# FFN in-projection by Strassen's seven block products from the third body on, out-projection in two halves

## The reference

```
gate, up = split(rms_norm(h, g) @ w_in, 2)      # w_in: 1024 x 5632, gate and up 2816 wide each
h = h + 0.5 * (silu(gate) * up) @ w_out         # w_out: 2816 x 1024
```

## Time and profile before

| | |
|---|---|
| runs of the kernel before (median) | 1895.05 us |
| the profiled execution, own time | 1895.18 us |
| its span, first to last instruction | 1893.4 us |
| TensorE busy | 1866.8 us, 99% |
| weight loads busy (beside TensorE) | 1536.2 us, 81% |
| VectorE busy | 927.1 us, 49% |
| ScalarE busy | 718.8 us, 38% |
| GpSimd busy | 24.5 us, 1% |
| granted TensorE clock, mean | 0.994 |
| DMA | 174.36 MB, 92 GB/s |

### The profile page before, as it was taken

How to read it: one execution, slowest core, us unless ns; L and a number is a source line. 1 busy time by engine, 2 the same in 40 slices (tenths; PEclk the granted TensorE clock), 3 DMA queues, 4 the chain that set the end, 5 groups by cost and what they waited for, 6 DMA issues and landing times.

```text
span 1893.4 us, 24130 instructions
## 1 busy us (share of the span) xinstructions
PE 1866.8 (99%) x8779; PEld 1536.2 (81%) x8779; DVE 927.1 (49%) x1336; ACT 718.8 (38%) x1177; POOL 24.5 (1%) x44
## 2 busy tenths in 40 slices
PE   9999999999998999999999999999999999999998
PEld 7888888877776888888888888888877788888888
DVE  5444434347886544444334444433478644444332
ACT  5232323336775432323233222323378432322332
POOL 1000000000000000000000000000000000000000
PEclk9999999999999999999999999999998999999999
DMA  4222223321111332222333222223311222232332
GB/s 167 98 91 100 94 87 105 125 89 56 57 56 34 101 99 89 100 100 78 109 105 109 100 97 92 94 92 102 123 56 53 71 97 92 100 100 82 98 102 86
DMA packets 55881, 174.36 MB, mean 92 GB/s; under 512 B 6672, under 2 KB 9232, under 8 KB 55824
## 3 DMA queue, kind: packets, MB, share of 16 engines
q1 hardware_dynamic: 55680, 173.57, 27.9%
q10 hardware_dynamic: 144, 0.03, 0.0%
HBM read 171.48 MB, written 2.10 MB: 92 GB/s over the span
## 4 chain that ended last, share of the span: by engine, by line
PE 95%; ACT 3%; DVE 1%; issue 1%; DMA 0%; POOL 0%; SPq 0%; DVEq 0%; POOLq 0%; ACTq 0%
PE bank L432 90%; PE bank L772 1%; PE bank L785 1%; ACT scratch L1316 1%; ACT w_hi L989 0%; PE bank L884 0%; ACT wide_hi L1272 0%; ACT wide_hi L1264 0%; PE bank L458 0%; DVE w_lo L1390 0%; PE bank L495 0%; PE bank L501 0%; PE bank L492 0%; DMA scratch<-x_dram 0%; PE bank L773 0%
## 5 line engine op out<-in xcount | busy, mean ns | idle before, releaser
L1390 DVE TENSOR_TENSOR w_lo<-raw,w_hi 128x1024 fp32r<-128x1024 f32 (+1 forms) x343 | 392.4, 1144 | 822.1 <-ACT w_hi L989 821.1
L989 ACT ACTIVATE w_hi<-raw 128x1024 fp32r<-128x1024 f32 (+1 forms) x343 | 341.3, 995 | 848.8 <-PE bank L432 846.3
L432 PE MATMUL bank<-u_hi,w_hi 128*128 128x512 f32 (+1 forms) x1592 | 631.1, 396 | 0.3 <-DVE w_lo L1390 0.3
L432 PE MATMUL bank<-u_hi,w_lo 128*128 128x512 f32 (+1 forms) x1592 | 620.9, 390 | 0.0
L432 PE MATMUL bank<-u_lo,w_hi 128*128 128x512 f32 (+1 forms) x1592 | 620.8, 390 | 0.0
L432 PEld LDWEIGHTS bank<-u_hi,w_lo 128*128 128x128 f32 (+1 forms) x1592 | 298.6, 188 | 63.9
L432 PEld LDWEIGHTS bank<-u_hi,w_hi 128*128 128x128 f32 (+1 forms) x1592 | 299.0, 188 | 61.0 <-issue 1.1
L432 PEld LDWEIGHTS bank<-u_lo,w_hi 128*128 128x128 f32 (+1 forms) x1592 | 298.9, 188 | 59.3 <-issue 1.0
L432 PE MATMUL bank<-wide_hi,w_hi 128*128 128x512 f32 (+1 forms) x816 | 317.6, 389 | 0.7 <-issue 0.4
L432 PE MATMUL bank<-wide_lo,w_hi 128*128 128x512 f32 (+1 forms) x816 | 315.7, 387 | 0.0
L432 PE MATMUL bank<-wide_hi,w_lo 128*128 128x512 f32 (+1 forms) x816 | 315.6, 387 | 0.0
(11 more groups left out here) (186 smaller groups left out, 1293.1 us busy)
## 6 DMA issues: line engine op xcount, KB each, us to landing
raw<-ffn_in_dram SPq DMA_DIRECT2D x175, 512.0 KB, 3.2
raw<-ffn_out_dram SPq DMA_DIRECT2D x128, 384.0 KB, 3.0
raw<-mix_w_dram SPq DMA_DIRECT2D x51, 512.0 KB, 3.2
y_dram<-raw SPq DMA_DIRECT2D x8, 256.0 KB, 2.7
scratch<-x_dram SPq DMA_DIRECT2D x2, 512.0 KB, 7.8
raw<-ffn_in_dram SPq DMA_DIRECT2D x2, 256.0 KB, 3.9
scratch<-x_dram SPq DMA_DIRECT2D x2, 256.0 KB, 4.2
sq<-x_dram SPq DMA_DIRECT2D x1, 512.0 KB, 9.6
```

The costliest lines, as they stand in the source:

```text
L432: mm = pe.matmul(out, a, b, start=first and k == 0, stop=last and k == n - 1)
L989: act.activation(w_hi[:, slot, 0:cols], raw[:, (base + r) % RAW, 0:cols], ACT.Copy)\
L1390: dve.tensor_tensor(w_lo[:, s, 0:cols], raw[:, r, 0:cols], f32(w_hi[:, s, 0:cols]), ALU.subtract).then_inc(w_ready, 1)
```

## The change

The first two bodies of each FFN stay. From the third on a body is computed by Strassen's scheme in the form with seven products (Winograd's variant). The k axis is cut in halves (features 0 to 511 and 512 to 1023), the tokens in halves of 256, and the two feature tiles of a side are the other halves. For each side (gate, then up) there are seven block products of 128 output features, 512 of k and 256 tokens, so 12 matmuls of 256 columns each. The token operands B11 to T4 (eight blocks, seven of them kept rounded) are made once for each FFN from h, the gain and `rstd_row`, one pair of k-tiles at a time through the one buffer `sums` (`mixed_inputs` on VectorE, `mix_tokens` on GpSimd, `mixed_split` on ScalarE, `mixed_lo` on VectorE). The weight operands S1 to S4 are sums and differences of weight blocks, made on GpSimd for every side of every body (`mix_weights`), and all seven weight operands are split as 128 x 512 blocks, one side ahead (`block_split` on ScalarE, `block_lo` on VectorE). Three partial results are copied out by ScalarE (`parts`), and VectorE adds them to the corners. Since the token operands carry `rstd_row`, the scaling behind the products goes. The seven products go to three banks a side.

`wide_hi` and `wide_lo` no longer have room for 22 tiles beside the mixed tokens, so the FFN is done in two parts: bodies 0 to 5 and their half of the out-projection (12 k-tiles, added to h, `h_mid`), then bodies 6 to 10 and theirs (10 k-tiles). Each half has four units for a pair of output tiles. The last pair of the kernel has 10 k-tiles in its halves of tokens instead of 22, and some of its transposes and sums come behind it. Smaller buffers move: `decay`, `diag` and `warm` share memory with others.

```diff
+PLAIN_BODIES = 2
+PART_BODIES = (6, 5)
+PART_KBS = ([range(0, 3), range(3, 6), range(6, 9), range(9, 12)], [range(0, 3), range(3, 6), range(6, 8), range(8, 10)])
+A11, A12, S1, S2, S3, S4, A22 = range(7)
@@ SP @@
+                def load_blocks(i, part, after=None):
+                    for r in range(IN_UNITS):
+                        if after is not None:
+                            sp.wait_ge(w_ready, after + r + 1)
+                        else:
+                            pair = BLOCK_PAIRS * f + 2 * (i - 1 - PLAIN_BODIES) + r // 2
+                            sp.wait_ge(block_ready, 7 * pair + (5, 7)[r % 2])
+                        load((rb + r) % RAW, ffn_in[f, i, r], UNIT)
@@ GpSimd @@
+            def mix_tokens(f, kb):
+                n = 3 * (4 * f + kb)
+                pool.wait_ge(mixed_in, 4 * f + kb + 1)
+                b = [mixed_src[:, j, :] for j in range(8)]
+                in_turn(n + 1, pool.tensor_tensor(b[T1], b[B12], b[B11], ALU.subtract), mixed_sum)
+                in_turn(n + 2, pool.tensor_tensor(mixed_src[:, T2:T3 + 1, :],
+                                                  mixed_src[:, B22:B22 + 1, :].to_broadcast([P, 2, HALF_TOK]),
+                                                  mixed_src[:, T1:B12 + 1:B12 - T1, :], ALU.subtract), mixed_sum)
+                in_turn(n + 3, pool.tensor_tensor(b[T4], b[B21], b[T2], ALU.subtract), mixed_sum)
+            def mix_weights(f, i, side, part):
...
+                for k, a, b, op in ((S1, x21, x22, ALU.add), (S2, four(sum_block(S1)), x11, ALU.subtract),
+                                    (S3, x11, x21, ALU.subtract), (S4, x12, four(sum_block(S2)), ALU.subtract)):
+                    if first:
+                        pool.wait_ge(mixed_ready, 4 * (f + 1))
+                    else:
+                        pool.wait_ge(block_ready, 7 * (pair - 1) + k + 1)
+                    in_turn(4 * pair + k - S1 + 1, pool.tensor_tensor(four(sum_block(k)), a, b, op), block_sum)
@@ TensorE @@
+            def block_body(f, i, part):
...
+                    if first and side == 0:
+                        pe.wait_ge(mixed_ready, 4 * (f + 1))
...
+                    for k, j, chain in ((A11, B11, 0), (S1, T1, 2), (S2, T2, 0), (A12, B21, 1), (S3, T3, 0),
+                                        (S4, B22, 2), (A22, T4, 0)):
+                        pe.wait_ge(block_ready, 7 * pair + k + 1)
+                        if k in (S2, S4, S3):
+                            pe.wait_ge(part_copied, 3 * pair + {S2: 1, S4: 2, S3: 3}[k])
+                        if k == A22:
+                            pe.wait_ge(corner_added, 3 * pair + 2)
+                        begins = k in (A11, S1, A12)
+                        out = bank[banks[chain]][:, 0:HALF_TOK]
+                        hi, lo = block_slot(f, side, k, False), block_slot(f, side, k, True)
+                        for kb in range(4):
+                            at = slice(kb * P, (kb + 1) * P)
+                            b_hi, b_lo = mixed(wide_hi, kb, j), mixed(wide_lo, kb, j)
+                            for n, (a, b) in enumerate(((hi[:, at], b_hi), (hi[:, at], b_lo), (lo[:, at], b_hi))):
+                                mm = pe.matmul(out, a, b, start=begins and kb == 0 and n == 0,
+                                               stop=kb == 3 and n == 2, skip_group_check=not begins)
+                        mm.then_inc(block_used, 1)
@@ ScalarE, the second plain body @@
+                        if i == 1:
+                            mixed_split(f, r)
+                        if i == 1 and r == 3:
+                            prologue(f, 4)
                         if r == 3:
                             for c in range(2):
+                                act.wait_ge(prod_ready, 2 * PLAIN_BODIES * f + 2 * i + c + 1)
+            def mixed_split(f, kb):
+                act.wait_ge(mixed_sum, 3 * (4 * f + kb) + 3)
+                act.activation(mixed(wide_hi, kb, 0, 7), sums[:, 0:MIXED], ACT.Copy).then_inc(mixed_hi, 1)
+            def prologue(f, r):
+                for k in ((), (), (A11,), (A12,), (S1, S2, S3, S4, A22))[r]:
+                    block_split(f, PLAIN_BODIES, 0, k, 0,
+                                base + {A11: 6, S1: 6, A12: 7, S2: 7, S3: 8, S4: 8, A22: 8}[k])
@@ ScalarE, a block body @@
+                    ahead(A11)
+                    for m, (used, chain) in enumerate(((1, 0), (2, 2), (3, 0))):
+                        act.wait_ge(block_used, 7 * pair + used)
+                        if type(i) is not int or pair >= 1:
+                            act.wait_ge(corner_added, 3 * (pair - 1) + (1, 2, 3)[m])
+                        act.activation(parts[:, m, :], bank[banks[chain]][:, 0:HALF_TOK], ACT.Copy)\
+                           .then_inc(part_copied, 1)
+                        ahead((A12, S1, S2)[m])
+                    ahead(S3)
+                    ahead(S4)
...
+                    else:
+                        ahead(A22)
+                        local = 2 * (i - PART_FIRST[part])
+                        for t in range(2):
+                            act.wait_ge(block_prod, 3 * body + (2, 3)[t])
+                            act.activation(dyn(wide_hi, (local + t) * SEQ), up_sums[:, t, :, :], ACT.Copy)\
+                               .then_inc(a_hi_ready, 1)
@@ VectorE, the plain bodies @@
+                        if i == 1:
+                            mixed_lo(f, r)
+                            if r < 3:
+                                mixed_inputs(f, nn, r + 1)
                         if r == 3:
...
+                            if i == 1:
+                                for k in (A12, S1, S2, S3, S4, A22):
+                                    block_lo(f, PLAIN_BODIES, 0, k, 0)
...
+                            if first:
+                                mixed_inputs(f, nn, 0)
+            def mixed_inputs(f, nn, kb):
+                if kb:
+                    dve.wait_ge(mixed_ready, 4 * f + kb)
+                elif f:
+                    dve.wait_ge(block_ready, 7 * BLOCK_PAIRS * f)
...
+            def mixed_lo(f, kb):
+                dve.wait_ge(mixed_hi, 4 * f + kb + 1)
+                dve.tensor_tensor(mixed(wide_lo, kb, 0, 7), sums[:, 0:MIXED], f32(mixed(wide_hi, kb, 0, 7)),
+                                  ALU.subtract).then_inc(mixed_ready, 1)
@@ VectorE, a block body @@
+                    for k in (A11, A12, S1):
+                        ahead(k)
+                    if side == 0 and (type(i) is not int or body >= 1):
+                        dve.wait_ge(block_prod, 3 * body)
+                    add(4, 1, 1, 0, 0)
+                    ahead(S2)
+                    add(5, 2, 0, 1, 1)
+                    ahead(S3)
+                    add(6, 3, 2, 0, 1)
+                    ahead(S4)
+                    ahead(A22)
+                    if side == 1:
+                        dve.wait_ge(block_silu, 3 * body + 3)
+                        dve.wait_ge(corner_added, 3 * pair + 3)
+                        dve.tensor_tensor(to[:, 1, 1, :], to[:, 1, 1, :], gate_sums[:, 1, 1, :], ALU.mult)\
+                           .then_inc(block_prod, 1)
+                        dve.tensor_tensor(to[:, 0, :, :], to[:, 0, :, :], gate_sums[:, 0, :, :], ALU.mult)\
+                           .then_inc(block_prod, 1)
+                        dve.wait_ge(block_used, 7 * pair + 7)
+                        dve.tensor_tensor(to[:, 1, 0, :], bank[banks[0]][:, 0:HALF_TOK], gate_sums[:, 1, 0, :],
+                                          ALU.mult).then_inc(block_prod, 1)
...
@@ TensorE, a half of the out-projection @@
+            def out_part(f, part, nn):
+                pe.wait_ge(a_ready, tiles - 2)
+                for mp in range(KB // 2):
+                    if mp >= 2:
+                        pe.wait_ge(*((h_mid, 8 * f + 2 * mp - 2) if part == 0 else (h_ready, 8 * nn + 2 * mp - 2)))
+                    for k in range(OUT_PAIR_UNITS):
+                        pe.wait_ge(w_ready, c + u + 1)
+                        if mp == 0 and k == OUT_PAIR_UNITS - 1:
+                            pe.wait_ge(a_ready, tiles)
```

622 lines of the change are left out of this document (416 added, 206 removed).

## The result

The changed kernel takes **2115.0 us** (2112.03 to 2120.29, four runs) against 1893.0 (1889.35 to 1897.22, four runs) for the kernel before: a ratio of **1.118** [1.116, 1.120]. The forecast was 1999 with a range of 1890 to 2065. The sign was right, the size was not: the change costs 222 us, not 104. One execution of a later version, the second of the run with both orders, took 2503.0 us at a granted clock of 0.674 and is left out everywhere, so that run stands on a single time. The profiled execution has a span of 2114.6 us (before: 1893.4) and a mean granted clock of 0.938 (before: 0.994).

What follows compares the result with a forecast made beforehand. The prediction took TensorE's matmul stream to bound the kernel (99% busy, 95% of the chain). It summed 1895.2 + 1.4 (block bodies) + 104.8 (mixing and first block bodies) - 2.4 (last pair) = 1999 us, range 1890 to 2065.

Steps and rivals of the forecast that it cites:

- Term 1: The 36 block bodies: 21.8 us each against 21.76, the seventh product's gain eaten by holes; +1.4 us (-57.6 to +84).
- the chain of the queues: Block bodies: ScalarE's copy stands behind roundings awaiting VectorE's products, so TensorE waits 0.73 us before the gate side's third product.
- the lock: Shared port of VectorE and GpSimd: each blocks the other for a whole instruction; took block bodies from 20.9 to 21.8 us.
- in the row the VectorE operation ran undelayed though it came later, so mostly VectorE wins: Block bodies: a profile row of a GpSimd pow meeting a VectorE subtraction, used to settle on 21.8 us a body.
- both of the later meetings: Block bodies: GpSimd's S3 delays VectorE's S4 split by 0.6 us; its S4 sum may delay the products 1.15 more.
- Rival 3: GpSimd saturates the port: sums of 1.45 us or more, 2054 us, at 1.7 us 2125; clock might drop too; 12%.
- Term 2: Each FFN's token mixing hole 16.5, first block body 8.0, clock drop 1.7 us: four times, +104.8 us (62 to 148).
- What was put at no cost at the middle of an FFN: Out-projection in two halves: splits, residuals and the second half's first block body lie under matmuls, adding no time.
- Term 3: Last pair, 10 k-tiles instead of 22 in 256-column halves, with its transpose tail: together -2.4 us.
- Rival 1: The lock doesn't bind, only the queues' order chain: bodies 20.9 us, prologues 24.2, total 1959 us; 20%.
- full matmul rate: Block bodies at 20.16 us each with no holes, within the rival where the lock doesn't bind: total 1932 us.
- Rival 2: The token mixing chain is hidden, only the first block body's 8 us is left: 1867 us, faster; 14%.

Runs made afterwards that it cites:

- the run with both orders: Changed kernel with roundings behind the next body's first copy and the second body's activation work ahead of the last mixing step: 2001.3 us, one execution.
- the copy moved: Changed kernel with ScalarE's two roundings of a block body behind the first copy of the next body's gate side: 2020.4 us, ratio 1.070.
- the filled hole: Changed kernel plus 24 unread matmuls ahead of the wait for ScalarE's copy in the 28 inner block bodies: 2071.1 us, ratio 1.094.
- The changed order of the second body: Changed kernel with the second plain body's activation work ahead of the last mixing step on VectorE and ScalarE: 2081.3 us, ratio 1.102.
- The short mixing: Changed kernel with GpSimd's three differences of token blocks in each mixing round made over 8 columns only: 2078.2 us, ratio 1.100.
- the run with short sums: Changed kernel with GpSimd's four weight-block sums made over a quarter of their columns, all waits kept: 1970.4 us, ratio 1.043.
- the run with short sums and the copy first: Changed kernel with GpSimd's weight sums over a quarter of their columns and roundings behind the next body's first copy: 1941.6 us, ratio 1.026.
- three plain bodies: Changed kernel with three plain bodies, mixing spread over the second and third, and roundings behind the next body's first copy: 1941.5 us, ratio 1.026.
- The best version here: Changed kernel with three plain bodies, roundings behind the first copy, weight sums (one split later) and mixing differences on VectorE: 1879.8 us, ratio 0.9935.

## Why the prediction was wrong in size, and where it was right

**Term 1 (block bodies, +1.4 us) is the step that failed.** By the bodies measured it is 36 x (20.16 - 21.76) + 28 x 5.3 = +91, which is 89 of the 116 us that were missing: 28 x 3.6 = 100 for the holes in inner bodies, where 36 times 1.6 (21.8 - 20.16) had been put in, and 48 for slow steps, where nothing had. The ingredients were right: steps of 0.120, the chain of the queues, the lock. What failed is "in the row the VectorE operation ran undelayed though it came later, so mostly VectorE wins". In the changed kernel the operation that started first went through, and the kernel's own waits put GpSimd first at 99 of the 108 splits of `w_lo` from sums. Why the row shows it the other way round (the pow of 4 elements started 0.3 us ahead and was the one delayed) stays open.

Take the inner body above and count from the end of the up side's product 6 (826.36), as the working did. The third corner add starts 1.15 us behind it (827.51) and not 0.16, because S3's split in front of it was held; S4's split loses 0.98 and the first product 1.08. VectorE's second product ends at 5.8 us instead of 2.84, the copy at 7.9 instead of 5.05. TensorE wants it at 4.32, so the hole is 3.5 and not 0.73. The working had named both of the later meetings (0.6, and 1.15 more) and settled at 0.9 for the lock; they and S3's come to 3.1, less 0.2 in the other steps. The Trainium skill (SBUF — State Buffer, SBUF: two separate sides) says that the loser is blocked for the whole instruction of the other; the trace agrees (the earlier trace rows and the timeline above).

With the copy moved, a body of the second part takes 21.7 us with the lock still on. The lock makes VectorE late by itself; the order chain hands that to TensorE.

**The clock inside term 1.** No drop was reckoned in the bodies, since shorter holes had left the clock full. Holes of 3.4 us brought one behind 25 of 28 inner bodies: 44 us by the filled hole, 48 by counting the slow steps. Rival 3 had named this ("Holes in every body might then drop the clock too"), but tied it to sums of 1.45 us or more. The sums take 1.3 alone, near the 1.2 taken; that its 2054 to 2125 takes in the measured 2115 is luck, since the time came by another way, delays in series in front of one copy.

**Term 2 (+104.8) was right in kind and a quarter too small.** 17.6 for 16.5 us at the mixing; in the first block body 14.6 us for 8.0 + 1.7. Of these, in the second FFN, about 9.0 are the hole at the copy, 1.3 that at a weight split, and 4.3 the slow steps in two stretches, one behind each long hole, where one stretch of 1.7 was reckoned. 4 x (17.6 + 14.6) = 129. The changed order of the second body took most of the hole at the copy away, as that step had it. The short mixing took 6.7 of the 17.6 us, which fits a serial chain in which VectorE and ScalarE have the larger share. What was put at no cost at the middle of an FFN cost nothing: the first block body of the second part takes 20.2 us.

**Term 3** (-2.4) was not tested by itself. 91 + 129 - 2.4 is 217 or 218 of the 221 us; the rest is not assigned.

**The rivals.** Rival 1 (the order chain alone, 1959) is the run with short sums, 1970, where an inner body's hole is 0.9 us against the 0.73 of the working; its full matmul rate (1932) is seen in the run with short sums and the copy first, 1941.6. Rival 2 (mixing hidden) is what three plain bodies make; its 1867 for the unchanged plan did not come, since even with GpSimd's differences cut to 8 columns the wait was 11.0 us.

The best version here has 32 block bodies, so the step of 0.120 leaves 32 x 1.6 = 51 us to the seventh product, and the version keeps 12.7 us of them (1892.5 - 1879.8). Of what is lost, the first block bodies take most: 27.0 us each on average for 20.16, 27 of the 38 us or so. That less work on VectorE there brings the time back was not tried.

## What to carry to other kernels

When a scheme trades matmuls for sums, count for each queue not only how much it has to do but what stands in front of the one instruction that TensorE waits for; here moving two roundings behind a copy was worth 95 us, and moving eight sums a body to the engine with more work 57 more. An engine that waits for a buffer of another starts in a fixed phase to it, so a shared port is met at the same place in body after body (99 of 108 splits here): look who holds it at that phase. And price a hole with what follows it: where slow steps lie behind it, filling it with useless matmuls can be cheaper than leaving it (44 us here).
